# Moving the split matmul operands of a two-block transformer kernel to other byte offsets of SBUF

## What is computed

```
y = (silu(h @ ffn_w_gate) * (h @ ffn_w_up)) @ ffn_w_down            # gated MLP, hidden 3584
y = sum over top-2 experts e: w_e * ((silu(h @ G[e]) * (h @ U[e])) @ D[e])   # hidden 3584
mixed = g0 * (y_attn @ w_br_attn) + g1 * (y_hyena @ w_br_hyena) + g2 * (y_gla @ w_br_gla)
k, v = rmsnorm(mem) @ wk, rmsnorm(mem) @ wv                          # 256 memory tokens
h = h + square(relu(rmsnorm(h) @ mlp_w1)) @ mlp_w2                   # hidden 4096
```

## The kernel before

| operand | before |
|---|---|
| `slots`, `slots_low`, `w_hi` (a tile of 128 columns begins at 128 or 640) | 128 |
| `x_hi`, `x_lo` | 128 |
| `branch_hi` (two) | 352 |
| `o_attn_low`, `o_hyena_low`, `o_gla_low` | 320 |
| `memory_hi`, `memory_lo` | 384 |
| `hidden_hi`, `hidden_lo` of the gated MLP | 448 |
| the same of the two later MLPs | 320 |
| the same of the experts; `w_hi_more` | 128 |
| `res`, `eye` / `ones` / `zeros` | 128 / 672 / 160 |

## Time and profile before

### The profile page before, as it was taken

One profiled execution on the slowest core, in us unless ns is written; L12 is line 12 of the kernel. 1 busy time (PEld: TensorE's weight loads), 2 busy tenths in 40 slices (PEclk: granted clock), 3 DMA queues, 4 the chain that ended last, 5 costly groups with the idle time before them and its releaser, 6 DMA issues. The chain is left out here.

```text
span 3016.6 us, 43738 instructions
## 1 busy us (share of the span) xinstructions
PE 2841.6 (94%) x17891; PEld 2527.3 (84%) x17891; DVE 2004.5 (66%) x2003; ACT 1513.7 (50%) x1456; POOL 68.8 (2%) x55
## 2 busy tenths in 40 slices
PE   5899999699999999999998989999999899999999
PEld 5799998588888888888885778999899788989898
DVE  6555565588888888888885556566555565665554
ACT  3443354376667766677762426443434226343432
POOL 1000000000000000000000110000000100000000
PEclk8899999699999999999998999999999899999999
DMA  6155540299999999999995333444355343444352
GB/s 186 61 178 182 182 141 29 91 367 334 376 333 352 355 334 375 333 354 353 334 374 157 127 101 103 144 157 145 99 190 185 116 126 101 143 144 131 128 188 104
DMA packets 365124, 619.40 MB, mean 205 GB/s; under 512 B 14664, under 2 KB 201126, under 8 KB 363700
## 3 DMA queue, kind: packets, MB, share of 16 engines
q1 hardware_dynamic: 363432, 611.77, 59.0%
q10 hardware_dynamic: 1550, 5.57, 0.5%
HBM read 611.93 MB, written 5.37 MB: 205 GB/s over the span
## 5 line engine op out<-in xcount | busy, mean ns | idle before, releaser
L354 DVE TENSOR_TENSOR slots_low<-slots,w_hi 128x2048 fp32r<-128x2048 f32 x240 | 549.5, 2293 | 396.2 <-ACT w_hi L343 396.1
L343 ACT ACTIVATE w_hi<-slots 128x2048 fp32r<-128x2048 f32 x240 | 452.1, 1888 | 359.4 <-PE ps L927 186.7
L1253 DVE TENSOR_TENSOR slots_low<-slots,w_hi 128x2048 fp32r<-128x2048 f32 x224 | 503.9, 2285 | 65.2 <-ACT w_hi L1204 65.2
L456 PE MATMUL ps<-x_hi,w_hi 128*128 128x256 f32 x1520 | 447.1, 294 | 51.4 <-DVE x_lo L536 26.7
L456 PE MATMUL ps<-x_lo,w_hi 128*128 128x256 f32 x1520 | 440.5, 290 | 0.0
L456 PE MATMUL ps<-x_hi,slots_low 128*128 128x256 f32 x1520 | 440.2, 290 | 0.0
L1204 ACT ACTIVATE w_hi<-slots 128x2048 fp32r<-128x2048 f32 x224 | 415.8, 1908 | 0.4 <-DMA slots<-in_moe_w_up_dram 0.3
L456 PEld LDWEIGHTS ps<-x_hi,w_hi 128*128 128x128 f32 x1520 | 302.7, 199 | 59.3 <-issue 51.8
L1137 PE MATMUL ps<-slots_low,x_hi 128*128 128x512 f32 x896 | 350.0, 391 | 0.0
L456 PEld LDWEIGHTS ps<-x_lo,w_hi 128*128 128x128 f32 x1520 | 303.0, 199 | 0.3
L456 PEld LDWEIGHTS ps<-x_hi,slots_low 128*128 128x128 f32 x1520 | 302.1, 199 | 0.0
(11 more groups left out here) (536 smaller groups left out, 5373.8 us busy)
## 6 DMA issues: line engine op xcount, KB each, us to landing
slots<-in_moe_w_gate_dram SPq DMA_DIRECT2D x112, 1024.0 KB, 5.1
slots<-in_moe_w_up_dram SPq DMA_DIRECT2D x112, 1024.0 KB, 5.2
slots<-in_moe_w_down_dram SPq DMA_DIRECT2D x112, 1024.0 KB, 5.0
slots<-in_mlp_w_dram SPq DMA_DIRECT2D x64, 1024.0 KB, 5.2
slots<-in_w_in_dram SPq DMA_DIRECT2D x54, 1024.0 KB, 5.3
slots<-in_ffn_w_gate_dram SPq DMA_DIRECT2D x14, 1024.0 KB, 5.0
slots<-in_ffn_w_up_dram SPq DMA_DIRECT2D x14, 1024.0 KB, 5.1
slots<-in_ffn_w_down_dram SPq DMA_DIRECT2D x14, 1024.0 KB, 4.8
```

Source lines behind the costliest of these rows:

```text
L343: act.activation(w_hi[:, s.buffer, 0:s.kt * s.cols], slots[:, s.slot, 0:s.kt * s.cols], ACT.Copy).then_inc(w_hi_done, 1)
L354: dve.tensor_tensor(slots_low[:, s.slot, 0:n], slots[:, s.slot, 0:n], w_hi[:, s.buffer, 0:n].bitcast(F32), ALU.subtract).then_inc(w_lo_don ...
L456: mm = pe.matmul(b[:, t * T:(t + 1) * T], w, xx[:, k, :], **flags)
L1253: dve.tensor_tensor(low[i % NS], raw[i % NS], his[i % R].bitcast(F32), ALU.subtract).then_inc(lo_done, 1)
```

## The change

No instruction is added, removed or moved between engines. A helper `home(c, at)` reserves as many bytes as bring the next tensor to the byte `at` modulo 1024. Some small tensors are allocated earlier, so that x needs no gap, and in the experts' router two scratch tensors are freed earlier, since the larger addresses would not fit otherwise (the largest end before was byte 229344 in that stage).

```diff
+ROW = 1024
+MOVING = 320
+HIDDEN_GATED = 256
+STATIONARY = 960
...
+        def home(c, at):
+            gap = (at - -(-nc.sbuf_base // 32) * 32) % ROW
+            if gap:
+                sb(c, "gap", [P, gap // 4])
+
         w_hi = sb(ctx, "w_hi", [P, NHI, 2048], F32R)
+        K = {"inv_freq": sb(ctx, "inv_freq", list(CONST["inv_freq"].shape))}
+        junk = sb(ctx, "junk", [P, 8])
+        filter_size = sb(ctx, "filter_size", [P, 2, 16])
+        home(ctx, MOVING)
         xh = sb(ctx, "x_hi", [P, KD, T], F32R)
         xl = sb(ctx, "x_lo", [P, KD, T], F32R)
...
                 tg, tu, sg, hid = (sb(c, n, [P, 2, T]) for n in ("gate_scaled", "up_scaled", "activated", "hidden"))
+                home(c, HIDDEN_GATED if gated else MOVING)
                 hth, htl = sb(c, "hidden_hi", [P, 2, 2, T], F32R), sb(c, "hidden_lo", [P, 2, 2, T], F32R)
...
                 sg, hid = sb(c, "activated", [P, W]), sb(c, "hidden", [P, W])
+                home(c, STATIONARY)
                 hth, htl = sb(c, "hidden_hi", [P, W], F32R), sb(c, "hidden_lo", [P, W], F32R)
...
                     mixed = sb(c1, "mixed", [P, KD, T])
+                    home(c1, MOVING)
                     bh = [sb(c1, "branch_hi", [P, 4, T], F32R) for _ in range(2)]
...
+                    home(c1, MOVING)
                     mh, ml = sb(c1, "memory_hi", [P, KD, T], F32R), sb(c1, "memory_lo", [P, KD, T], F32R)
```

More of the change, by code:

```diff
@@ L220, in program @@
         res = sb(ctx, "res", [P, KD, T])
-        K = {}
         ALWAYS = ("eye", "blocks64", "rot32", "rot16", "twice0", "twice1", "causal_add", "later", "gla_keep", "inv_freq")
-        for name in ALWAYS:
+        for name in ALWAYS[:-1]:
             K[name] = sb(ctx, name, list(CONST[name].shape))
@@ L226, in program @@
         zeros = sb(ctx, "zeros", [P, 256], BF16)
-        junk = sb(ctx, "junk", [P, 8])
         eye = K["eye"]
@@ L1586, in layer @@
             with ExitStack() as c:
+                home(c, MOVING)
                 (oa, oa_low), (oh_, oh_low), (og, og_low) = (pinned(c, n, [P, 4, T]) for n in ("o_attn", "o_hyena", "o_gla"))
@@ L2539, in program @@
                 with ExitStack() as c1:
-                    xg, sq = sb(c1, "gained", [P, KD, T]), sb(c1, "squares", [P, KD, T])
                     htm = sb(c1, "by_token", [P, TT, D])
@@ L2544, in program @@
                     sel_r = sb(c1, "row_select_r", list(CONST["row_select"].shape), F32R)
-                    with stage("gained", "squared", "turned", "summed", "scored", "step", "rooted") as (block, gained, squared, turned, summed, scored, step, rooted):
+                    with ExitStack() as c2, stage("gained", "squared", "turned", "summed", "scored", "step", "rooted") as (block, gained, squared, turned, summed, scored, step, rooted):
+                        xg, sq = sb(c2, "gained", [P, KD, T]), sb(c2, "squares", [P, KD, T])
                         @block.scalar
@@ L2722, in program @@
         memT = sb(ctx, "memory", [P, KD, T])
-        filter_size = sb(ctx, "filter_size", [P, 2, 16])
         for name in ("axial_cos", "axial_sin", "gla_sum", "dft", "idft"):
```

## The result

The kernel after the change takes 2995.32 us (median of four runs, 2988.92 to 3001.26); beside it the kernel before took 3014.82 (four runs, 3012.11 to 3021.54). The ratio is 0.9933, with a 95% interval of 0.9913 to 0.9953: faster by 0.7%, 19.5 us, where 49 us were forecast. 2995 lies above the range of 2947 to 2993. The profiled execution of after took 2988.92 us, with a span of 2987.1, so it is 29.5 us shorter than that of before (3016.6).

A forecast was written before the change was run, and what follows sets the result against it. TensorE, busy 94%, was taken as the bound through the distance between matmul starts. Terms -46 (part 1), -0.7 (gated hidden), 0 (L461), -2.5 (experts) made -49 us from 3016.6, so 2968 us; range 2947 to 2993.

The forecast's parts named there:

- second rival: Side chains or loads end last, L456's waits grow by 25 us, half of part 1 is lost: 2993 us, chance 0.07.
- control pair: `branch_hi` at 352 (283 ns) and `o_attn_low` at 320 (278): same tiles, same line, only the byte differs.
- first product of the experts: L1137, x stationary at 320: 1920 matmuls at +2.6 ns, +5.0 us; 768 with `w_hi_more` taken as 0.
- slower rival: Experts' stationary x makes two stalls per 512-column matmul; at +25 ns each, 3033 us; chance 0.03.
- experts' second product: L1159, hidden to 960: 1216 matmuls save 6.4 ns, -7.8 us; 128 with `w_hi_more` cost +0.3; near 220 ns.
- last rival: The slower rival; its argument noted L935's distance as worse than 0, though better at 256 columns; chance 0.03.
- part 1: L456 and L927: x, `branch_hi`, memory to 320; 7930 matmuls at 6.2 ns, 49.2 us, less 3 back: -46 us.
- gated hidden: Gated MLP's hidden from 448 to 256: 672 matmuls at 116.8 ns between its neighbours, -0.7 us, bounds -6.0 to +1.4.
- L461: x and memory stationary at 320, weights moving at 128: some 790 matmuls, taken as 0, bounds -1.6 to +2.0 us.
- The 3 us that were given back for side chains: In `linear`, rotations, decays and square roots beside the matmuls would show under shorter cover: 3 us off part 1's gain.
- first rival: Distances without a row (gated hidden, experts) come out at no loss, nothing given back: 2942 us, chance 0.09.
- the experts' -2.5 us: L1137 and L1159 together, operands moved from 128: -2.5 us, ends -16.5 and +7.3.

The follow-up runs named there:

- again: The changed kernel once more, unaltered: 2996.72 us, ratio 0.9936 to the kernel before.
- sweep: Separate kernel, TensorE alone: moving or stationary operand at 16 places in steps of 32 bytes; 113.4 to 120 ns for 256 columns.
- experts128: Changed kernel with the experts' x, hidden and `w_hi_more` back at byte 128: 2983.26 us, ratio 0.9886; repeated later, 2975.47 us, ratio 0.9876.
- entry: Separate kernel, TensorE alone: 72 sequences at 320 after pauses, none to four matmuls ahead, then 8-byte steps; 42 of 71 at the better spacing.
- shift: Separate kernel, TensorE alone: stationary and moving operands shifted together by 0 to 224 bytes; distance 0 gave 120.0 ns at multiples of 32.

## Why the prediction was wrong

**What held.** TensorE's distances were the right place to look: waits, DMA and the splitting took nothing back (the second rival), as the waits show. The distance between moving and stationary is the cause, and the control pair in the earlier trace rows was read rightly. x at 320 can run at 113.4 ns. The first product of the experts cost +5.2 us against +5.0, but only the sum agrees, by luck: the 1920 matmuls without `w_hi_more` cost +3.0 us (+4.5 in `again`) where +5.0 was forecast, the 768 with it +2.2 where 0 was. L935 stayed at 229.0 ns. The small float32 tensors cost nothing (all else: -0.3 us). The slower rival didn't come: 512 columns on x at 320 reached 229.1 ns with `w_hi`, far from the 246 at which it would have decided.

**The step with the wrong sign: the experts' second product.** "If 512 columns save the same 6.4 ns as 256 do" carried a price over from one shape to another, with ends of 0 and a gain; no loss was allowed for, although the same text priced L1137 with a loss at the neighbouring distance. It measured +7.4 us instead of -7.5, 233.2 ns instead of about 220. What should have warned: both shapes have rows for the distances 0 and 320, and of these 0 is the better for 512 columns (226.5 against 229.0 ns) and the worse for 256 (120.0 against 117.9). The forecast noted this under its last rival and took the price over all the same. Two shapes that disagree about the places that both have can't share a table. Nor was the distance one modulo 512: by `sweep`, 192 and 448 are the same place, and the matmuls with `w_hi_more` at 448, priced at 0, came to 232.8 ns, much as L1173 at 192 did (233.2).

**The mis-sized term: part 1, 39.5 instead of 46 us.** The 6.2 ns a matmul came from slabs at the better of two spacings. Over all of x in `linear` after gained 4.5 ns (119.89 to 115.36); memory stayed at 117.3 ns, and branches and memory together gained 2.1 us, where 6.2 ns each would be 4.7. The row that shows the second spacing was in the trace of before, in the first slab of the second stack's MLP, next to the ones that I took:

```profile
2178.50 0.28 PE L942 MATMUL ps<-hidden_lo,w_hi 128*128 128x256 f32 x1
...
2183.92 0.28 PE L942 MATMUL ps<-hidden_hi,slots_low 128*128 128x256 f32 x1
```
5.42/46 = 117.8 ns, with hidden at 320, at the line where the earlier trace rows have 113.6. The 14 slabs behind it came straight from x at 128 and were at 113.6; the last one, behind a wait, was at 118 again. So the earlier trace rows hold the price of one way of coming in, not of a distance. In `linear` the sequences of x are cut by waits and other instructions, as the two stretches above show, and in after 1907 of 4286 distances stayed above 115 ns.

**Smaller terms.** The gated hidden went to 118.9 instead of 116.8 ns: the mean of two neighbours said nothing, since the map isn't smooth. L461 gained 2.7 us, beyond its bound of 1.6: its distance, 320, is 64 modulo 256 and has the two spacings as well, and the row at 448 that priced it shows the worse one alone (at 115 ns or less were 317 of 781 distances without a wait, before 43). The 3 us that were given back for side chains had no cause; no wait grew.

**The range.** Its lower half was spent on unknown distances that might be free, and its upper end of 2993 on a rival without a row. Neither held the case that came: the experts losing 12.6 us together with a part of x at the worse spacing. The experts' low end was added up wrongly besides: -16.5 us leaves out the +5.0 of L1137, with it -11.5, and the first rival's time would be 2947 us instead of 2942.

**The size itself.** With x, branches, memory and hidden as moving operands at a place where hardly any but the better spacing came, and the experts left where they were, part 1 is 46.7 us (1091.3 to 1044.6) and the whole -51.0 us (span 2965.6). So the price (5.9 ns for each of the 7930, against 6.2) was nearly right for that kernel, which wasn't the one forecast. That its 2967 us are nearly the forecast 2968 is in part luck: the experts' -2.5 us isn't in it, and the gated and the later hidden have -2.7 and -1.1 instead of -0.7 and 0.

**The median.** The ledger accounts for 19.5 us of the miss (29.7 instead of 49.2); the medians miss by 10 us more, since they differ by 19.5 us and the profiled spans by 29.5. The span of before (3016.6) lies above the median of its four runs (3014.82), and the profiled execution of after is the shortest of its four. The others are up to 12 us longer; that more of their matmuls ran at 117.8 ns is argued from `experts128`, where two executions are seen to differ so, and not shown for them.

The Trainium skill's rule that was weighed (TensorE: Matmul & The Clock Gate, Part 2, Step-by-step: two independent read ports, and a distance of N/2.4 + 2.5 ns) is not borne out by `sweep`, `entry` and `shift`: 113.3 to 122.4 ns for 256 columns and 226.6 to 234.3 for 512, with nothing altered but the operands' bytes and the pauses. Its figures would be 109.2 and 215.8 ns; no place reached them. The zeros of the earlier trace rows have 109 ns, but in bfloat16 and with weight loads of 98 ns beside the matmuls, where the loads of the float32r tiles take 186 ns or more; so the forecast's bound of 109 ns was no price for float32r.

## What to carry to other kernels

Where TensorE is busy throughout, look at the distance between starts and not at busy time, and make a table of it by shape, operand and place; a price holds for its own shape alone. Read all slabs of a group before pricing from one: two means in one group, each steady over dozens of matmuls, are two spacings that keep themselves up, and how a sequence is entered decides between them. Then look for a placement that has one spacing only (here, with stationary tiles at multiples of 32 bytes, a distance of 112 bytes modulo 256 for 256 float32r columns, 0 for 512): it is worth the mean. The scatter was smaller too (4.7 against 14 us over five runs each); but the kernel before scattered by 13 us over nine runs beside them, with x at a place of one spacing, so that the two spacings make the scatter isn't shown.

## What the runs showed of the hardware

- The distance of two matmuls depends on where the moving operand lies against the stationary one, modulo 256 bytes: 113.3 to 122.4 ns for 256 columns, 226.6 to 234.3 ns for 512, at the full clock. At a granted clock of 0.50 distance 0 has 213.0 ns, which is 256 columns at 1.2 GHz: no stall.
- At the distances 64 and 192 two spacings exist, 113.3 and 117.8 ns, and a sequence keeps one of them: 42 of 71 starts after a pause, with none to four matmuls ahead, fell on the better one at 192. In the kernel most stretches show the same one in each execution, but a whole MLP differed between two executions (117.7 and 113.7 ns).
- At the distance 112 a sequence settles at 113.3 (47 of 48), but at 116.7 to 120 ns when the stationary tile begins 16 bytes off a multiple of 32.
- Places 8 bytes off a multiple of 16 are mostly the worse ones, up to 122.4 ns. The Trainium skill's page SBUF — State Buffer, Specifications (TRN2), gives lines of 16 bytes and a penalty for each crossing. The direction agrees with these rows; how large the penalty is and which reads cross, no run here shows.
- Why the two columns of the map differ, and why 112 is free of the second spacing, stays open.
